# State space mixer of a hybrid decoder step on one core: running sums as rows, spread by one-hot products in three row groups; output products alternate between column halves

## The reference, cut to what matters

```python
acs = jnp.cumsum(dt * a.reshape(G, J), axis=2)
xdt = x * dt[..., None]
seg = acs[:, :, :, None] - acs[:, :, None, :]
decay = jnp.exp(jnp.where(causal, seg, -jnp.inf))
cb = jnp.einsum('bclgn,bcsgn->bclsg', cc, bc)
y_diag = jnp.einsum('bclsg,bclsgj,bcsgjp->bclgjp', cb, decay, xdt)
```

## Time and profile before

| what | value |
|---|---|
| median of the runs | 2019.89 us |
| the three runs | 2020.94, 2015.41, 2019.89 us |
| span of the profiled execution | 2015.7 us |
| PE, DVE, ACT, POOL busy | 97%, 62%, 46%, 50% |
| mean granted TensorE clock over the span | 0.986 |
| the state space mixer | about 460 to 845 us of the span |

### The profile page before, as it was taken

How to read it: one execution, slowest core, us unless ns; L and a number is a source line. 1 busy time by engine, 2 the same in 40 slices (tenths; PEclk the granted TensorE clock), 3 DMA queues, 4 the chain that set the end, 5 groups by cost and what they waited for, 6 DMA issues and landing times.

```text
span 2015.7 us, 35615 instructions
## 1 busy us (share of the span) xinstructions
PE 1951.5 (97%) x13890; PEld 1763.9 (88%) x13890; DVE 1244.4 (62%) x2220; ACT 930.6 (46%) x1557; POOL 1008.8 (50%) x1249
## 2 busy tenths in 40 slices
PE   7999999999999999999999999999999999999997
PEld 5998989798888988897889999999998889989976
DVE  5988342426887787755147777777454157874552
ACT  3676522334555555342354444443243347674333
POOL 4776704026555655250356666566631337776602
PEclk8999999999999999999999999999999999999998
DMA  4444476535444544487353444444586344445870
GB/s 130 149 147 135 135 250 231 208 105 174 124 116 132 151 132 140 138 297 241 113 170 108 130 130 130 137 136 146 165 313 211 132 148 141 135 148 166 292 231 27
DMA packets 332615, 324.64 MB, mean 161 GB/s; under 512 B 19768, under 2 KB 313056, under 8 KB 332448
## 3 DMA queue, kind: packets, MB, share of 16 engines
q1 hardware_dynamic: 330944, 321.49, 49.8%
q10 hardware_dynamic: 1504, 0.87, 0.2%
HBM read 292.16 MB, written 29.61 MB: 160 GB/s over the span
## 4 chain that ended last, share of the span: by engine, by line
PE 75%; DVE 14%; ACT 5%; issue 2%; DMA 2%; POOL 1%; SPq 1%; DVEq 0%; ACTq 0%
PE ps L773 10%; PE ps L774 10%; PE ps L778 10%; PE ps L1458 5%; PE ps L1467 4%; PE ps L1261 3%; PE ps L1524 2%; PE ps L888 2%; PE ps L763 2%; PE ps L765 2%; PE ps L764 2%; ACT wh L1713 2%; DVE work L2543 2%; PE ps L1602 1%; PE ps L1541 1%
## 5 line engine op out<-in xcount | busy, mean ns | idle before, releaser
L1693 POOL TENSOR_TENSOR wl<-raw,wh 128x256 fp32r<-128x256 f32 x1216 | 1003.3, 860 | 979.1 <-ACT wh L1713 978.9
L1713 ACT ACTIVATE wh<-raw 128x1024 fp32r<-128x1024 f32 x304 | 311.8, 1053 | 202.1 <-PE ps L778 49.8
L773 PE MATMUL ps<-Hh,wh 128*128 128x320 f32 x1200 | 372.2, 324 | 2.8 <-DVE work L2563 0.9
L774 PE MATMUL ps<-Hl,wh 128*128 128x320 f32 x1200 | 360.4, 314 | 0.0
L773 PEld LDWEIGHTS ps<-Hh,wh 128*128 128x128 f32 x1200 | 230.0, 192 | 11.3 <-DVE work L2427 2.3
L774 PEld LDWEIGHTS ps<-Hl,wh 128*128 128x128 f32 x1200 | 230.4, 192 | 2.1
L2258 DVE TENSOR_SCALAR work<-ps 128x512 f32<-128x512 f32 (+8 forms) x220 | 100.3, 474 | 170.9 <-PE ps L871 39.8
L778 PE MATMUL ps<-Hh,wl 128*128 128x320 f32 x1200 | 201.1, 310 | 0.0
L778 PEld LDWEIGHTS ps<-Hh,wl 128*128 128x128 f32 x1200 | 183.2, 189 | 0.1
L773 PE MATMUL ps<-Oh,wh 128*128 128x320 f32 x512 | 152.2, 310 | 3.7 <-DVE Ol L3004 3.7
L774 PE MATMUL ps<-Ol,wh 128*128 128x320 f32 x512 | 151.1, 308 | 0.0
(11 more groups left out here) (439 smaller groups left out, 3922.0 us busy)
## 6 DMA issues: line engine op xcount, KB each, us to landing
raw<-rg_w_in SPq DMA_DIRECT2D x128, 256.0 KB, 3.5
raw<-hg_w_in SPq DMA_DIRECT2D x128, 256.0 KB, 4.8
raw<-ssd_w_in SPq DMA_DIRECT2D x96, 256.0 KB, 3.9
work<-cache_mem_k SPq DMA_DIRECT2D x40, 512.0 KB, 6.3
work<-cache_mem_v SPq DMA_DIRECT2D x40, 512.0 KB, 5.1
raw<-rg_w_out SPq DMA_DIRECT2D x64, 256.0 KB, 3.6
raw<-x_w_k SPq DMA_DIRECT2D x64, 256.0 KB, 3.6
raw<-x_w_v SPq DMA_DIRECT2D x64, 256.0 KB, 3.7
```

Source lines behind the costliest of these rows:

```text
L773: pe.matmul(ps[:, bank, 0:n], high(half, k), mh[:, k, 0:n], start=(k == 0), stop=False)
L774: pe.matmul(ps[:, bank, 0:n], high(half, k), ml[:, k, 0:n], start=False, stop=False)
L1693: ins = pool.tensor_tensor(out, src, wh[:, parted(n) % HALVES, r:r + 2].bitcast(F32), ALU.subtract)
L1713: act.activation(wh[:, nx.n % HALVES], raw[:, slot, :, half * P:(half + 1) * P], ACT.Copy).then_inc(hi_ready, 1)
```

## The change

Three things change. `sums_of_steps` also makes the running sums with heads on partitions: `sd_acs` holds row 32T + head, 128 tokens wide; this takes three more products on TensorE and two more copies on ScalarE. `decays(j)` no longer makes the sums again: the stationary operand is one column of the identity, restricted to the 32 rows of piece T and repeated 128 times, and the moving one is `sd_acs` on the same 32 rows. The loop goes over heads and inside over T, and it waits for `sd_xt_read`, `sd_xs_read` and `sd_bt_read` all together, ahead of its first product, and for `sd_cb_read` behind its last. In `outputs` the loops are turned round: for each T both halves n follow each other, and then the two products of the samples. The tile `sd_acs` needs room in SBUF, and the scratch area that the program sets aside for dynamic DMA is made smaller.

```diff
+        sd_acs = sb("sd_acs", [96, P])
...
                     for T in range(2):
                         pe.matmul(ps[:, 5, 32 * T:32 * T + 32], upper[:], sd_ta[:, 1, T, :], start=True, stop=True)
                         pe.matmul(ps[:, 5, 96 + 32 * T:128 + 32 * T], later[:], sd_ta[:, 1, T, :], start=True, stop=True)
+                        pe.matmul(ps[32 * T:32 * T + 32, 5, 256:384], sd_ta[:, 1, T, :], upper[:], start=True, stop=True)
                     pe.matmul(ps[:, 5, 192:224], ones[:], sd_ta[:, 1, 1, :], start=True, stop=True)
+                    pe.matmul(ps[64:96, 5, 256:320], sd_ta[64:P, 1, 2, :], s_causal[64:P], start=True, stop=True)
...
                 def decays(j):
-                    def dta(T, h, n, rows=slice(0, P)):
-                        return sd_ta[rows, 1, T, 4 * j + h:4 * j + h + 1].broadcast_to([rows.stop - rows.start, n])
-
-                    for T, bank, read in ((0, 4, "sd_xt_read"), (1, 5, "sd_xs_read")):
-                        pe.wait_ge(*past(read, j + 1))
-                        for h in range(4):
-                            mm = pe.matmul(ps[:, bank, h * P:(h + 1) * P], dta(T, h, P), upper[:], start=True, stop=True)
-                        mm.then_inc(S(f"sd_seg{T}_full"), 1)
+
+                    pe.wait_ge(*past("sd_xt_read", j + 1))
+                    pe.wait_ge(*past("sd_xs_read", j + 1))
                     pe.wait_ge(*past("sd_bt_read", j + 1))
+                    for h in range(4):
+                        for T in range(3):
+                            rows, w, c = slice(32 * T, 32 * T + 32), (P, P, 64)[T], 32 * T + 4 * j + h
+                            one = ident[rows, c:c + 1].broadcast_to([32, P])
+                            mm = pe.matmul(ps[:, 4 + T, h * w:(h + 1) * w], one, sd_acs[rows, 0:w], start=True, stop=True)
+                            if h == 3:
+                                mm.then_inc(S(f"sd_seg{T}_full"), 1)
                     pe.wait_ge(*past("sd_cb_read", j + 1))
-                    for h in range(4):
-                        mm = pe.matmul(ps[:, 6, h * 64:(h + 1) * 64], dta(2, h, P, sm), s_causal[sm], start=True, stop=True)
-                    mm.then_inc(S("sd_seg2_full"), 1)
...
+                    for T in range(2):
+                        for n in range(2):
+                            h, rows = 2 * t + n, slice(64 * n, 64 * n + 64)
+                            pe.matmul(ps[rows, bank, T * P:(T + 1) * P], sd_xt[:, T, h, :], sd_e[:, T, h, :], start=True, stop=True)
                     for n in range(2):
-                        h = 2 * t + n
-                        rows = slice(64 * n, 64 * n + 64)
-                        for T in range(2):
-                            pe.matmul(ps[rows, bank, T * P:(T + 1) * P], sd_xt[:, T, h, :], sd_e[:, T, h, :], start=True, stop=True)
+                        h, rows = 2 * t + n, slice(64 * n, 64 * n + 64)
                         pe.matmul(ps[rows, bank, 256:320], sd_xt[sm, 2, h, :], sd_e[sm, 2, h, 0:64], start=True, stop=True)
...
+                    steps.did(act.activation(sd_acs[0:64], ps[0:64, 5, 256:384], ACT.Copy))
+                    steps.did(act.activation(sd_acs[64:96, 0:64], ps[64:96, 5, 256:320], ACT.Copy))
```

More of the change, by code:

```diff
@@ L3049 @@
     from concourse.bass_utils import run_bass_kernel_spmd as _run
-    nc = _bacc.Bacc("TRN2", target_bir_lowering=False, num_devices=1)
+    nc = _bacc.Bacc("TRN2", target_bir_lowering=False, num_devices=1, dynamic_dma_scratch_size=1024)
     arrays = {n: np.ascontiguousarray(inputs[n]) for n in INPUTS}
```

## The result

The changed kernel takes 2022.38 us, the median of 20 runs (2017.67 to 2027.04), the kernel before 2018.69 us in its 20 (2011.18 to 2022.68). The ratio of the new time to the old is 1.0025 with a 95% interval of 1.0016 to 1.0034: slower by about 5 us. (The ratios are worked out from all runs of both kernels and need not be the quotient of the two medians, which is 1.0018 here.) The predicted 2019 us was 3.4 us too low, inside the range of 2006 to 2030, and the slowdown of 0.25% stays under the 0.3% that was called no change. But it is a loss whose interval leaves out 1, and the forecast was a small gain: the direction was wrong. The profiled execution has a span of 2020.8 us at a mean granted clock of 0.982, 5.1 us more than before.

A forecast was written before the change was run, and what follows sets the result against it. VectorE's chain to the gate, beside a TensorE 97% busy, was taken to absorb most of the 25.8 us removed: -2.6 us for the groups plus 2 for the clock, -0.6 on the 2019.9 median, so 2019 us, range 2006 to 2030.

The forecast's parts named there:

- the chain of VectorE: From VectorE's first difference to the gate's end and TensorE's next step: 24.72 us, with no TensorE work the change shortens.
- the clock: Granted clock falls to half behind longer gate waits: 0 to four further falls of 1.5 us each, taken as +2 us.
- sizes on TensorE: Per group `decays` takes 1.19 us, saving 1.71; each `outputs` call takes 0.84 us, saving 0.83.
- The rival in which the row groups don't overlap: In `decays`, VectorE starts 1.8 us later in all groups: 11 us, 2031 us; chance 0.11.
- the decays' saving goes nowhere: At `take_z`, TensorE waits 1.9 to 2.0 us for ScalarE's copy in seven groups and goes on 0.20 us later.
- The rivals in which all or half comes through: Of the TensorE time removed: all 25.8 us saved, 1994 us, chance 0.07; or half, 2010 us, chance 0.14.
- but the gate is read 0.20 later: In steps 1, 2 and 7 TensorE's gate wait grows to 2.6 us; step 2 ends 0.20 us later.
- groups 2 to 5: Steps 3 to 6, at the two `take_out` pieces: shift -0.5 us each, -2.0 us over four.
- the clock falls at the new waits: Rival: clock falls at most gate waits and half the `take_z` waits, costing 7 to 10 us: 2028 us; chance 0.13.
- Group 0 and group 7: First group shifts +1.0 us by ScalarE's copies and later `decays`; last gains 2.0 us from both savings and an earlier cast.
- The sum: Over all groups -2.6 us without the clock, +2 us for the clock, together -0.6 us.

The follow-up runs named there:

- decays_only: Changed kernel with the loops of `outputs` as before, so only the new sums and decays: ratio 0.9996 to the kernel before, 2016.68 us.
- all_best_order: Changed kernel with `gate` first in steps 0 to 2 and 7, `pack` last, ScalarE's copy for `take_z` ahead of the cast: 1.0013 to before, 2018.39 us.
- outputs_only: Kernel before with the new loops of `outputs`, sums and decays as before: ratio 1.0023 to the kernel before, 2022.65 us.
- second_output_only: Kernel before with the new loops for `outputs(j, 1)` alone: ratio 1.0001 to the kernel before, 2016.19 us.
- all_pack_late: Changed kernel with `pack(i)` moved behind `gate(i)` on VectorE: ratio 1.0004 to the kernel before, 2018.54 us.
- all_with_filler: Changed kernel with twelve unread products on TensorE ahead of the gate waits of steps 1, 2 and 7: ratio 0.9989 to before, 2014.59 us.
- all_pack_late_filler: Changed kernel with `pack` behind the gate and nine unread products ahead of the three gate waits: ratio 0.9974 to before, 2010.98 us.
- all_gate_first: Changed kernel with `gate(i)` ahead of `outputs(j, 0)` on VectorE: ratio 0.9972 to the kernel before, 2013.53 us.
- outputs_copy_early: Kernel before with new `outputs` loops, gate early in steps 1, 2, 7, `pack` late, `last_rows` and first `take_out` copies early: 0.9967 to before, 2011.31 us.
- all_copy_early: all_best_order with `last_rows` ahead of the convolution's last tap and first `take_out` copy ahead of `squares_of`: ratio 0.9954 to before, 2006.20 us.
- run 24: Not a run: in "Three row groups of 32 rows run 24 fp32 records" the word run is a verb and 24 counts records.

## Why the prediction was wrong, and what in it was right

The number lay 3.4 us from the measured one and inside the range, but a gain of 0.6 us was forecast and a loss of about 5 us came. Two terms of its sum failed, the chain of VectorE and the clock.

**Right: sizes on TensorE.** `decays` took 1.09 us to the start of what follows (1.19 said), `outputs` 0.85 (0.84), VectorE began 1.19 us behind the first record (1.29), ScalarE's two further copies cost 0.53 us (0.5). The rival in which the row groups don't overlap is out. (Its delay was worked out from the wrong record: the last product of T = 0 is the tenth of twelve, so its record is the 20th and not the 22nd, and 12 x 0.112 + 0.2 makes 1.5 us and not 1.8.)

**Right: the decays' saving goes nowhere.** The wait at `take_z` came out at 1.7 us in six groups (1.9 to 2.0 in seven said), and decays_only ran at 0.9996. The rivals in which all or half comes through are out; all_best_order shows that the cast ahead of the copy was the reason for the wait, but that shortening it alone doesn't help, since the next consumer waits in its place. With that one moved too, what the decays add is the 0.13% above, within the noise.

**Failed: "but the gate is read 0.20 later".** The prediction took the chain of 24.72 us as fixed, since it "holds no TensorE work that the change shortens". Its length was not its own. The shorter `outputs(j, 0)` brought ScalarE's cast and GpSimd's subtractions 0.8 us nearer, into VectorE's small copies, and the chain grew by 0.6 us in each of seven groups. So the groups 2 to 5 did not gain 0.5 each: +0.20, +0.18, -0.17, -0.17. The groups in front of the gates, three and not the two that the sum counted, lost 0.6 more by it, and the gates' waits became 3.1 us and not 2.6. outputs_only has it, second_output_only and decays_only don't, all_pack_late takes most of it away, and its groups 2 to 5 gain what was forecast.

**Mis-sized: the clock, +2 us said.** The falls at the gates were foreseen, at 1.5 us each. All three came, and their price was 2.3 to 2.7 us each, since the clock stayed low for 6.8 us and not 3. The distance 1 to 2 has it without a fall in before: 44.44 - 41.19 - 0.60 = 2.65 us, or 2.5 against the run with filler. With before's one fall (42.72 - 41.19 = 1.5 us) taken off, the gates cost +6.2 us. This isn't a mistake apart from the first: in all_pack_late, where the waits are 2.4 us, near the 2.6 that were expected, each fall lasted 3.4 us and cost the 1.5 us that were said; at 3.1 us, in the changed kernel and in outputs_only, all six falls lasted 6.8 us. Why the length goes so stays open. There was a fourth at the wait for the running sums: from `turn(0)` to the first difference 5.88 us, and 4.50 in the same kernel with the filler, where the clock was full there; 1.4 us more. A fifth, at 830.1 us, lies in group 7. The rival "the clock falls at the new waits" named 7 to 10 us for this; 8.9 came, but not at `take_z`, where the clock fell in none of the groups of this profile. It did fall there once each in the profiles of all_with_filler, all_pack_late_filler, all_gate_first and outputs_copy_early, at or just behind waits of 1.8, 1.9, 3.8 and 3.0 us.

**Group 0 and group 7.** Without the clock, group 0 moved by 0.53 for the copies and 4.50 - 3.91 = 0.6 for `decays`, 1.1 (+1.0 said). Group 7 gained 0.9 us and not 2.0, but with the clock low from 830.1 to 833.5 us in it. In all_with_filler, where the clock fell only behind it, it takes 829.91 - 812.86 = 17.05 us, 2.2 less than before: the forecast of 2.0 was right, and the fall took 1.3 of it.

**The sum.** Without the clock: 1.1 + 3 x 0.6 + 0.04 - 2.2 = +0.7, where -2.6 was said. Clock: 6.2 + 1.4 + 1.3 = +8.9, where +2 was said. Together +9.6 in place of -0.6. The two profiled spans differ by 5.1 only, because the profiled run of the changed kernel came to its running sums 2.6 us earlier (494.62 against 497.24) and took 1.8 us less behind the `sums` of group 7, in code that the change leaves alone. Over 20 runs the ratio says 5 us. So the direction and the place are shown, and the 9.6 is what one execution had; where the clock falls differs between the profiles, and a single one doesn't give the mean. From VectorE's first difference of group 0 to the `sums` of group 7 the profiles have 330.1 us before, 337.1 in the changed kernel, 336.5 in outputs_only, 330.6 in decays_only, 330.2 in all_pack_late, 329.5 in all_with_filler, 325.3 with both and 321.6 in all_copy_early: by and large in the order of the ratios.

**Open.** That the copies and the addition are slowed by GpSimd is shown by when they meet and by moving either side, not by taking GpSimd's work away. How much of the 5 us is group 0's wait wasn't tried by itself. And second_output_only has 326.5 us in the stretch above, 3.6 less than before, while the whole kernel didn't get faster by anything that can be measured; but its profile is of the fastest of its 12 executions (2009.61 us, median 2016.19), and one profile can't say what the others had.

## What to carry to other kernels

Time taken off a full engine ahead of a wait only lengthens the wait, and a longer wait on TensorE was paid again here, in the clock behind it. So look first at who is waited for next on each path, the arrival of weights among them, move that work earlier, and only then make the products shorter; here the same change went from 5 us of loss to some 8 us of gain that way. And an end that comes earlier also moves what it releases on the other engines: see whom those will meet.

## What the hardware showed

- Twelve products of 128 columns that nobody reads, put in a wait of 3.1 us, were worth 7 us over three such waits, since the clock stayed at 2.4 GHz.
- Waits of 3.1 us at the gate were followed by 6.8 us at 1.2 GHz in six of six cases, waits of 2.4 us by 3.4 us in three of three, waits of 1.5 us (all_best_order) by 3.4 us in three of three, waits of 1.7 us (second_output_only) in one of three, waits of 0.9 us in one of three, in the kernel before and in decays_only alike. A fall of 3.4 us cost 1.5 us, one of 6.8 us 2.3 to 2.7.
- Three row groups of 32 rows run 24 fp32 records in 1.1 us where 24 records on full or half rows took 2.90; two column halves halve a call of 1.67 us.
- Two copies of 12 columns on VectorE, 0.27 us together, took 0.60 us when GpSimd's subtraction had begun ahead of them.
